# Two norms' sums of squares: four chunks of the first post-norm and one more of the final norm handed to GpSimd

## The reference, cut to what matters

```python
def rms_norm(x, g):
    xf = x.astype(jnp.float32)
    y = xf * lax.rsqrt(jnp.mean(xf * xf, axis=-1, keepdims=True) + EPS)
    return (y * g.astype(jnp.float32)).astype(x.dtype)

hs = hs + rms_norm(mix, norm_mix_post[layer])      # "mixpost0" for layer 0
...
return rms_norm_2(h, final_g).astype(x.dtype)      # "final"
```

## Time and profile before

| | us |
|---|---|
| median of 3 runs | 1031.02 |
| lowest, highest | 1026.96, 1033.98 |
| the profiled execution | 1026.96 |
| its span | 1025.0 |
| TensorE busy in the span | 957.1 (93%) |
| VectorE busy | 541.4 (53%) |
| ScalarE busy | 413.8 (40%) |
| GpSimd busy | 174.6 (17%) |

### The profile page before, as it was taken

How to read it: one execution, slowest core, us unless ns; L and a number is a source line. 1 busy time by engine, 2 the same in 40 slices (tenths; PEclk the granted TensorE clock), 3 DMA queues, 4 the chain that set the end, 5 groups by cost and what they waited for, 6 DMA issues and landing times.

```text
span 1025.0 us, 16906 instructions
## 1 busy us (share of the span) xinstructions
PE 957.1 (93%) x6800; PEld 794.3 (77%) x6806; DVE 541.4 (53%) x999; ACT 413.8 (40%) x691; POOL 174.6 (17%) x234
## 2 busy tenths in 40 slices
PE   4799999999889999999998999979889999999986
PEld 3699999998777899999996999869645445544466
DVE  4755554446775665554437547764533433344267
ACT  4444333435654754344335546643211111111163
POOL 5233333122000533332110000002010000000013
PEclk8899999999898999999999999998899999999999
DMA  7425553467802435443562422118549999999921
GB/s 302 164 97 189 193 194 113 169 191 210 206 1 83 164 121 208 173 185 131 208 248 82 165 99 77 47 47 306 239 169 410 418 419 419 420 418 420 421 104 42
DMA packets 36798, 211.99 MB, mean 207 GB/s; under 512 B 2529, under 2 KB 16113, under 8 KB 17521
## 3 DMA queue, kind: packets, MB, share of 16 engines
q1 hardware_dynamic: 36720, 210.91, 54.6%
HBM read 209.83 MB, written 1.07 MB: 206 GB/s over the span
## 4 chain that ended last, share of the span: by engine, by line
PE 83%; DVE 9%; ACT 3%; POOL 2%; issue 2%; DMA 0%; DVEq 0%; POOLq 0%; ACTq 0%
PE ps L1316 49%; PE ps L1718 11%; PE ps L1732 6%; PE ps L1741 3%; DVE mix L1865 2%; PE ps L1308 2%; PE ps L1690 2%; PE ps L1691 1%; DVE wl L753 1%; DVE hs L577 1%; PE ps L1243 1%; PE ps L1251 1%; PE ps L1336 1%; PE ps L1676 1%; PE ps L1659 1%
## 5 line engine op out<-in xcount | busy, mean ns | idle before, releaser
L753 DVE TENSOR_TENSOR wl<-ring,wh 128x2048 fp32r<-128x2048 f32 (+3 forms) x104 | 205.5, 1978 | 185.1 <-ACT wh L743 185.1
L743 ACT ACTIVATE wh<-ring 128x2048 fp32r<-128x2048 f32 (+3 forms) x104 | 172.4, 1661 | 257.3 <-PE ps L1316 255.6
L1316 PE MATMUL ps<-xh,wh 128*128 128x256 f32 (+3 forms) x600 | 169.4, 282 | 1.3 <-DVE xl L2315 1.0
L1316 PE MATMUL ps<-xh,wl 128*128 128x256 f32 (+3 forms) x600 | 168.0, 280 | 0.0
L1316 PE MATMUL ps<-xl,wh 128*128 128x256 f32 (+3 forms) x600 | 167.8, 280 | 0.0
L1316 PEld LDWEIGHTS ps<-xh,wh 128*128 128x128 f32 (+3 forms) x600 | 111.3, 186 | 3.1 <-DVE xl L2315 1.2
L1316 PEld LDWEIGHTS ps<-xh,wl 128*128 128x128 f32 (+3 forms) x600 | 111.3, 186 | 0.1
L1316 PEld LDWEIGHTS ps<-xl,wh 128*128 128x128 f32 (+3 forms) x600 | 111.2, 185 | 0.0
L1316 PE MATMUL ps<-acth,wl 128*128 128x272 f32 (+1 forms) x352 | 100.1, 284 | 0.0
L1316 PE MATMUL ps<-actl,wh 128*128 128x272 f32 (+1 forms) x352 | 100.1, 284 | 0.0
L1316 PE MATMUL ps<-acth,wh 128*128 128x272 f32 (+1 forms) x352 | 100.0, 284 | 0.0
(11 more groups left out here) (426 smaller groups left out, 1874.3 us busy)
## 6 DMA issues: line engine op xcount, KB each, us to landing
wring<-in_w_eg SPq DMA_DIRECT2D x32, 2048.0 KB, 14.9
ring<-in_w_gu SPq DMA_DIRECT2D x22, 2048.0 KB, 8.1
wring<-in_w_ed SPq DMA_DIRECT2D x16, 2048.0 KB, 13.4
ring<-in_w_dn SPq DMA_DIRECT2D x16, 1408.0 KB, 6.0
ring<-in_w_z SPq DMA_DIRECT2D x7, 2048.0 KB, 7.7
ring<-in_w_out SPq DMA_DIRECT2D x4, 1152.0 KB, 5.9
ring<-in_w_q SPq DMA_DIRECT2D x8, 512.0 KB, 6.2
ring<-in_w_o SPq DMA_DIRECT2D x8, 512.0 KB, 16.2
```

The lines of the kernel that those rows point to most:

```text
L743: ins = act.activation(to, src, ACT.Copy)
L753: ins = dve.tensor_tensor(to, src, h.bitcast(F32), ALU.subtract)
L1316: ins = mm(o, p, q, start=first and n == 0, stop=last and n == 2)
```

## The change

The norm `mixpost0` is put into the table with 4 chunks: GpSimd adds the squares of chunks 0 to 3 behind its pool groups, and TensorE sums `sqsum` once, behind the matmuls of chunk 4, and then chunks 4 to 7 as before. The norm `final` has 7 chunks on GpSimd in place of 6, and ScalarE squares only the last. The diff:

```diff
-SUMMED = {"ffnpre0": 6, "ffnpost0": 7, "pre1": 6, "mixpost1": 7, "ffnpre1": 6, "ffnpost1": 7,
-          "norm2": 7, "ple": 6, "final": 6}
+SUMMED = {"mixpost0": 4, "ffnpre0": 6, "ffnpost0": 7, "pre1": 6, "mixpost1": 7, "ffnpre1": 6, "ffnpost1": 7,
+          "norm2": 7, "ple": 6, "final": 7}
...
             pool_groups(pool, chain, (0, 1), "p_pool")
+            sum_chunks(pool, "mixpost0", T)
             sum_chunks(pool, "ffnpre0", T)
...
-            for c in range(SUMMED["final"], KD):
-                wait_hs(act, 6, c)
-                square(act, "final", c, hs[:, c, N_META:], SEQ)
+            wait_hs(act, 6, KD - 1)
+            square(act, "final", KD - 1, hs[:, KD - 1, N_META:], SEQ)
             rsqrt(act, chain, "final", D, SEQ)
...
                 elif name == "final":
-                    pe.wait_ge(sem("sq_ready"), SQ0["final"] + c - summed + 1)
+                    pe.wait_ge(sem("sq_ready"), SQ0["final"] + 1)
```

## The result

| us | before | after |
|---|---|---|
| median of 20 runs each | 1026.99 | 1039.92 |
| lowest, highest | 1022.86, 1033.98 | 1031.18, 1052.39 |
| the profiled execution | 1026.96 | 1041.04 |
| its span | 1025.0 | 1039.3 |

The ratio after to before is 1.0108, 95% interval 1.0089 to 1.0128: slower by about 11 us, with an interval of 9 to 13. The medians of the table lie 12.9 us apart; the ratio is taken over more runs and leaves out the slow ones, of which 1052.39 is one. The forecast was +5.4 us. The forecast time, 1036.4, lies nearer to 1039.92 than that, because two misses work against each other: with more runs the median of before is 1026.99, not 1031.02, and the loss is twice the forecast.

A forecast was written before the change was run, and what follows sets the result against it. It took TensorE's work and waits to set the time (83% of the chain, VectorE 9%). 2.9 + 1.7 + 0.8 = +5.4 us on 1031.02 gave 1036.4 us, range 1030 to 1041 (its own case 1032 to 1040).

The forecast's parts named there:

- The mixer's wait, +2.9: Pool mixer's norm: TensorE's sum of sqsum waits for GpSimd's third add, starting at 36.95 instead of 34.06, +2.9 us.
- The order of the steps: Pool mixer: first split to 33.52, add 1 to 34.14, second split to 36.28, add 2 to 36.90, sum at 36.95.
- add 1: Pool mixer, GpSimd's second add: ready at 31.8 during VectorE's first split, ends 0.62 us after it, at 34.14.
- add 2: Pool mixer, GpSimd's third add: meets VectorE's second split and ends 0.62 us after it, at 36.90.
- The bounds (+0.1 and +3.2): Pool mixer's wait: +0.1 us if VectorE does not hold GpSimd, +3.2 us if both splits go first.
- The clock, +1.7: Behind the mixer's new 3.8 us TensorE pause: 3.4 us of work at half speed, costing 1.7 us.
- The bound, 4.6: Clock behind the mixer's pause: all that is left of the stage at low clock, 4.6 us more.
- The tail, +0.8: Kernel's end: GpSimd's multiply and add for chunk 6 start the last sums at 1017.55 instead of 1016.73, +0.8 us.
- The 1.37 us of removed sums are already in this: Pool mixer: TensorE's removed sums, 1.37 us, give nothing further because TensorE only arrives earlier at a wait.
- Rival D: From the mixer through the feed-forward block's first stage: clock not granted again, 13.8 us slower, 1044.8 us; chance 0.06.
- The base: Whole kernel: the +5.4 us was added to 1031.02, the median of three runs, 4.06 above the profiled execution.
- Slower by over 1%: Whole kernel's measured time: over 1% slower, chance 0.06; faster by over 1% had 0.02, within 1% had 0.92.

The follow-up runs named there:

- part 1: The kernel before with only mixpost0 changed, four chunks summed on GpSimd, final as before; 1.0115, 1039.63 us.
- part 1 and the code put back: part 1 plus three float32 matmuls of ones, read by nobody, in idle TensorE time ahead of the mixer; 1.0039, 1033.85 us.
- the three matmuls: Three float32 matmuls of ones in idle TensorE time ahead of the mixer; added alone to the kernel before 0.9985, to the whole change 1.0045.
- splits held back: part 1, with VectorE's two weight splits waiting for GpSimd's third add; 1.0077 against the kernel before.
- 240 more: The kernel before plus 120 one-column bf16 matmuls (240 instructions with their weight loads) in idle time ahead of the mixer; 1.0050, 1036.52 us.

## Why the prediction was right or wrong

**The mixer's wait, +2.9: right.** The sum of `sqsum` starts at 37.26, against 34.06, less 0.2 by which this execution runs late already (28.76 for GpSimd's first add, whose group ended at 27.88 + 0.70 = 28.58 before): +3.0. The order of the steps is the predicted one. The first split is moved (31.45), add 1 gets its turn between two queued splits, the second split, 2.85 in place of 2.28, waits for it, and add 2 stands to its end. Holding the splits back brings the sum to 34.15. The bounds (+0.1 and +3.2) held. The Trainium skill's exclusive lock (page "SBUF — State Buffer", section "SBUF: two separate sides") agrees: adds of 2.3 and 2.6 us beside the splits, 0.76 without.

**The clock, +1.7: the mechanism right, the term too small.** It cost 2.6 to 2.7 us, 8.69 us for work that takes 6.08. I had taken the length of low clock behind another pause, 3.4 us, from the earlier trace rows. Here the clock fell during the pause, and TensorE worked at 0.50 from 37.26 to about 42.3, 5 us. With part 1 and the code put back the same stretch took 44.61 - 36.84 = 7.77, a cost of 1.7, as forecast: there the granted clock was 1.00 until 38, 0.50 from 39 to 41 and 1.00 again from 42, so the low stretch met less work. Three of the four traces with this pause have 2.6 to 2.7, one has 1.7, and one row of before doesn't give the size. The bound, 4.6, held.

**The tail, +0.8: right.** 1.81 us against 1.04. VectorE's add of chunk 7 took 0.72 for 0.42, held by GpSimd's multiply, as foreseen.

**The step that failed** is one the prediction left unsaid: that a shift passes through the rest unchanged, and that the removed sums give back nothing more and take nothing. It wrote of the removed matmuls "The 1.37 us of removed sums are already in this". They also moved all of TensorE's later code by 12 instructions, and there the expert stage lost 5.1 us in the profiled execution, a pause of 3 us and low clock behind it, and about 6 by the ratios (1.0108 against 1.0045). By the ratios, 4.5 for the forecast's places and 6.3 for the code make the 11 us. By the two traces, the terms 3.0 + 2.6 + 0.8 = 6.4 and these 5.1 leave about 3 of the 14.3 us between the spans without a cause. The size of the code's cost is not fixed either: three pairs of kernels with and without the three matmuls differ by 6.3 (the change), 7.6 (part 1) and 10.4 us (part 1 with the splits held back), and the last trace shows only 4.7 of it at the experts. Rival D, dearer by the clock alone, had the right sign for the remainder and the wrong cause: the clock was back by 43.

**The base.** The prediction added its sum to the median of three runs. By 17 to 33 runs the median lies between 1026.99 and 1029.66, near the profiled execution's 1026.96. A sum made against one execution is better read as a difference; the time that it gives was near by luck: +5.4 on the 1026.99 of 20 runs would have been 1032.4, 7.5 below what was measured. The prediction also said that under 1% can't be told from no change; with these numbers of runs the intervals are 0.2 to 0.3% to each side.

**Slower by over 1%** had a chance of 0.06, all of it from D. It came out with the ratio just above that line.

**How the code comes in.** What is shown: pauses at "issue", where no semaphore, load or operand is waited for, come and go with the number of TensorE instructions ahead of the experts. Against before, that number is lower by 12 in the change, in part 1 and with the splits held back: pauses in each. It is higher by 0, 12, 20 (32 less 12) and 54 in the other kernels: none over 1.3 us, though with 54 the stage is longer by 2.8 us in short stops. And higher by 240: six. Each team begins with a branch past code for tokens that overflow (`extra`, a runtime `If` that is not taken here), so TensorE jumps ahead in its code there. The page of each kernel lists a queue that brings instructions, as here (56 and 0.92 in the kernel with 240 more, 55 and 0.90 in all others):

```profile
q8 instruction: 55, 0.90, 0.4%
```

55 packets, 0.90 MB, so 16 KB each. The Trainium skill has the rule (page "Runtime: NRT & Kernel Launch", section "Instruction fetch mechanics"): instructions come in 16 KiB blocks of 256, and "a taken branch whose target isn't in the current 2-page window forces a DMA fetch of the target page before execution can continue". The packet size agrees; how large the window is for TensorE no run here shows. By 256 to a block, 240 more is 16 fewer, next to the change's 12 fewer, and these are the kernels with pauses.

The record shows more than this likeness. The trace keeps the start and length of each of these packets. At 14 team heads of the four kernels with pauses TensorE stops for 1.8 us or more, counted from the start of one matmul to the start of the next, where 0.42 is usual. In all 14 it starts again 1.66 to 1.83 us after such a packet has ended. Six of them:

| kernel | last matmul starts | packet of 16 KB | TensorE starts again | after the packet's end |
|---|---|---|---|---|
| after | 788.90 | 789.80 to 790.79 | 792.51 | 1.72 |
| part 1 | 789.20 | 790.88 to 791.90 | 793.62 | 1.72 |
| part 1 | 824.33 | 823.53 to 824.62 | 826.28 | 1.66 |
| splits held back | 779.40 | 778.74 to 779.73 | 781.45 | 1.72 |
| before, 240 more | 782.73 | 782.36 to 783.40 | 785.06 | 1.66 |
| before, 240 more | 844.99 | 844.18 to 845.21 | 846.93 | 1.72 |

The table also says why a pause is near 2 us at one head and near 4 at another: the packet comes ahead of the last matmul in the short ones and behind it in the long ones. At the heads without a pause, in these kernels and in before, the packet comes after the next matmuls have begun, or has ended 1.9 us or more ahead of them. So TensorE waits for its instructions here, as far as times can show it. That the branch is what makes a block come late is argued, not shown: no run took the branch away, and which engine a packet is for isn't in the trace. What decides when the packet comes, and so how many pauses an execution has (one, four and three in kernels with the same TensorE program), stays open.

## What to carry to other kernels

Work handed to GpSimd beside VectorE's large two-input operations is done when those are, not when its operands are; put it ahead of them by a semaphore. Look at the granted clock behind every new TensorE pause: here those of 3.0 to 3.9 us, at the mixer and at the experts, were followed by work at 0.50, those near 2 us were not. A change that removes or adds a few instructions on an engine with runtime branches moves its later code: before reading a ratio of 1%, look for new idle at "issue" behind the branches, hold it against the instruction packets, and put the removed instructions back in idle time as a control. Take the change as a difference, and don't lean on a median of three runs.

## What was not expected of the hardware

Twelve TensorE instructions fewer, 700 us ahead, cost about 6 us in a stage that they don't belong to; 240 more cost about 5, and 12 more nothing that can be told. In each of 14 pauses there TensorE started again 1.7 to 1.8 us after a 16 KB instruction packet had ended. A pause of 2 to 4 us lengthened the distance of the following loads by 1.5 to 5.7 us, the longest ones by more than themselves, since the clock fell behind them. And nearly the same pause at the mixer (3.6 to 3.9 us) was followed by a clock cost of 2.6 to 2.7 us in three executions and 1.7 in a fourth.
